# Rotary turn, score banks, order of maxima and roots in the differential attention of a two-block transformer kernel

## What is computed

```python
def rope(x, pos):                       # halves of 32 within each head of 64
    x1, x2 = xf[..., :half], xf[..., half:]
    return jnp.concatenate([x1 * cos - x2 * sin, x2 * cos + x1 * sin], axis=-1)

def diff_attention_group(q, k, v, pos, layer, lambdas, subln):
    q, k = rope(...), rope(...)         # 8 heads, each with two q and two k of 64
    # per block of 128 queries: two softmaxes over the keys up to the query's chunk of 64
    p1 = masked_softmax(q1 @ k1.T * scale, mask); p2 = masked_softmax(q2 @ k2.T * scale, mask)
    o = (p1 - lam * p2) @ v
    o = rms_norm_2(o, subln) * (1.0 - lam_init)
```

## Time and profile before

| what | value |
|---|---|
| median of 3 runs | 2726.69 us (2720.05 to 2731.51) |
| the profiled execution | 2719.96 us, span of its instructions 2718.2 us |
| mean granted clock of PE | 0.976 |
| PE busy (matmuls) | 2572.1 us, 95% of the span |
| PEld busy (weight loads) | 2022.0 us, 74% |
| DVE busy | 1305.1 us, 48% |
| ACT busy | 878.3 us, 32% |
| POOL busy | 1074.5 us, 40% |
| the chain that ended last | PE 78%, DVE 14%, ACT 4% of the span |

### The profile page before, as it was taken

One profiled execution on the slowest core, in us unless ns is written; L12 is line 12 of the kernel. 1 busy time (PEld: TensorE's weight loads), 2 busy tenths in 40 slices (PEclk: granted clock), 3 DMA queues, 4 the chain that ended last, 5 costly groups with the idle time before them and its releaser, 6 DMA issues.

```text
span 2718.2 us, 30446 instructions
## 1 busy us (share of the span) xinstructions
PE 2572.1 (95%) x11830; PEld 2022.0 (74%) x11830; DVE 1305.1 (48%) x2013; ACT 878.3 (32%) x1354; POOL 1074.5 (40%) x841
## 2 busy tenths in 40 slices
PE   7999999999999999989988999999997789999998
PEld 6878676888788888766766677888885666788886
DVE  4225677533433321585756654585126765533301
ACT  3443245322222222224444533322233243322221
POOL 4322243644454445343222235454452331544442
PEclk9999999999999999999999999999997889999999
DMA  3111122222222223211111122222320011222232
GB/s 134 66 55 63 50 74 72 95 97 94 93 90 95 95 90 94 92 62 60 49 47 47 47 70 99 93 93 91 97 97 30 21 40 39 97 94 94 93 94 74
DMA packets 62575, 209.45 MB, mean 77 GB/s; under 512 B 6880, under 2 KB 9312, under 8 KB 62304
## 3 DMA queue, kind: packets, MB, share of 16 engines
q1 hardware_dynamic: 61424, 204.11, 23.0%
q10 hardware_dynamic: 1008, 3.40, 0.3%
HBM read 205.38 MB, written 2.10 MB: 76 GB/s over the span
## 4 chain that ended last, share of the span: by engine, by line
PE 78%; DVE 14%; ACT 4%; issue 2%; POOL 1%; DMA 0%; DVEq 0%; ACTq 0%; SPq 0%; POOLq 0%
PE ps L609 22%; PE ps L610 22%; PE ps L611 22%; DVE T L2012 1%; PE ps L630 1%; ACT A L1475 1%; PE ps L632 1%; PE ps L631 1%; DVE A L2311 1%; DVE small L2157 1%; PE ps L920 1%; DVE A L1901 1%; POOL w_lo L567 1%; PE ps L737 1%; PE ps L739 1%
## 5 line engine op out<-in xcount | busy, mean ns | idle before, releaser
L567 POOL TENSOR_TENSOR w_lo<-w_raw,w_hi 128x512 fp32r<-128x512 f32 (+4 forms) x822 | 1047.1, 1298 | 1578.2 <-ACT w_hi L1214 1578.2
L609 PE MATMUL ps<-H,w_hi 128*128 128x512 f32 x1880 | 765.4, 407 | 39.5 <-POOL w_lo L567 19.6
L610 PE MATMUL ps<-H,w_hi 128*128 128x512 f32 x1880 | 750.7, 399 | 0.0
L611 PE MATMUL ps<-H,w_lo 128*128 128x512 f32 x1880 | 750.4, 399 | 0.0
L1214 ACT CAST w_hi<-w_raw 128x1024 fp32r<-128x1024 f32 (+4 forms) x411 | 401.9, 983 | 540.7 <-DMA w_raw<-in_weights_dram 535.1
L609 PEld LDWEIGHTS ps<-H,w_hi 128*128 128x128 f32 x1880 | 358.4, 191 | 139.2 <-issue 37.3
L609 PE MATMUL ps<-split,w_hi 128*128 128x512 f32 x1034 | 419.2, 405 | 11.8 <-POOL w_lo L567 5.8
L611 PEld LDWEIGHTS ps<-H,w_lo 128*128 128x128 f32 x1880 | 357.4, 190 | 87.2
L610 PEld LDWEIGHTS ps<-H,w_hi 128*128 128x128 f32 x1880 | 358.5, 191 | 81.9 <-issue 1.4
L610 PE MATMUL ps<-split,w_hi 128*128 128x512 f32 x1034 | 412.5, 399 | 0.0
L611 PE MATMUL ps<-split,w_lo 128*128 128x512 f32 x1034 | 412.1, 399 | 0.0
(11 more groups left out here) (395 smaller groups left out, 2493.7 us busy)
## 6 DMA issues: line engine op xcount, KB each, us to landing
w_raw<-in_weights_dram SPq DMA_DIRECT2D x323, 512.0 KB, 3.6
w_raw<-in_weights_dram SPq DMA_DIRECT2D x48, 448.0 KB, 3.2
w_raw<-in_weights_dram SPq DMA_DIRECT2D x22, 256.0 KB, 2.6
X<-in_xt_dram SPq DMA_DIRECT2D x4, 512.0 KB, 7.6
out_dram<-A SPq DMA_DIRECT2D x8, 256.0 KB, 2.2
w_raw<-in_weights_dram SPq DMA_DIRECT2D x12, 128.0 KB, 2.0
w_raw<-in_weights_dram SPq DMA_DIRECT2D x6, 192.0 KB, 2.3
A<-in_w_gates_dram ACTq DMA_DIRECT2D x1, 1024.0 KB, 5.6
```

The lines of the kernel that those rows point to most:

```text
L567: sub = nc.gpsimd.tensor_tensor(w_lo[:, p % NS, c], w_raw[:, p % NS, c], w_hi[:, p % NS, c].bitcast(F32), ALU.subtract)
L609: mm_(ps[:, bank, :], r(wh), xh, start=(k == 0), stop=False)
L610: mm_(ps[:, bank, :], r(wh), xl, start=False, stop=False)
L611: mm = mm_(ps[:, bank, :], r(wl), xh, start=False, stop=(k == kt - 1))
```

## The change

The rotary turn is made by ACT: behind the copy of a tile, four copies of 32 rows each from the bank to `ROPE_T`, each group from its neighbour's rows, with a scale of -1 or 1; ACT waits for the turn before (`s_roped`) first. PE's `rotate`, its matrix, and the "rot" items of the fill are gone; DVE's turn waits for the copies (`s_qc`) and reads `ROPE_T` in place of bank 2. The fills become 3 a step in the scan stage and 5, 5, 5, 4 in the attention. The scores of a step go to two of three banks (4, 5, 2) in turn, and `scores(c)` waits for the first exponential of the step before only. DVE takes the maxima of step c + 1 ahead of the normalising of step c. The head's root and reciprocal are exp(-0.5 ln(x)) on ACT, with a load of a table set that holds both functions ahead of the loop; DVE's reciprocal is gone. The root of the gate norm stays a square root at the same place, and a wait for its sums that `root` has anyway stands in front of it once more. In the last layer only counts of semaphores change.

```diff
@@ -405,6 +401,10 @@
         YG = parts_at(BW_AT, BW_AT + 2048)
         YC = parts_at(13312, 13312 + 2048)
         YD = parts_at(5120, 7168)
+
+        def map_bank(c, a):
+
+            return (4, 5, 2)[(2 * c + a) % 3]
 
         def h_tile(i):
             return H32[:, i // 8, i % 8, :]
@@ -514,14 +514,11 @@
         DONE_B = steps_done(FILL_B, PATTERN_B, 16)
 
         def dqkv_items(p):
-            name = f"dqk{p}"
-            return [((name, 0), 8), ((name, 1), 8), (("rot", 4 * p), 1), ((name, 2), 8), (("rot", 4 * p + 1), 1),
-                    ((name, 3), 8), (("rot", 4 * p + 2), 1), (("part", p), 12), (("rot", 4 * p + 3), 1),
-                    ((f"dv{p}", 0), 4)]
-
-        SSM_FILL = (3, 3, 3, 4)
+            return [((f"dqk{p}", n), 8) for n in range(4)] + [((f"dv{p}", 0), 16)]
+
+        SSM_FILL = (3,)
         DONE_SSM = steps_done(dqkv_items(0) + dqkv_items(1), SSM_FILL, 32)
-        DIFF_FILL = (5,)
+        DIFF_FILL = (5, 5, 5, 4)
         _items = dqkv_items(2)
         _items.insert(1, (("cols", 0), 0))
         _items.insert(3, (("spread", 0), 0))
@@ -862,13 +859,6 @@
             products_bc(6)
             products_bc(7)
 
-            def rotate(i):
-                p, n = divmod(i, 4)
-                pe.wait_ge(s_qc, i + 1)
-                if i >= 1:
-                    pe.wait_ge(s_rotf, i)
-                mm_(ps[:, 2, :], con("rot64"), QD[p][:, n, :], start=True, stop=True).then_inc(s_rot, 1)
-
             def fill_dqkv(p):
                 for n in range(4):
                     yield from units((f"dqk{p}", n), HX)
@@ -876,14 +866,7 @@
                         norm_cols("gate", 7)
                     if p == 2 and n == 1:
                         norm_spread("gate", 7, RTG)
-                    if n:
-                        rotate(4 * p + n - 1)
-                        yield
-                for u, _ in enumerate(token_units((f"dv{p}", 0), HX)):
-                    yield
-                    if u == 11:
-                        rotate(4 * p + 3)
-                        yield
+                yield from token_units((f"dv{p}", 0), HX)
 
             def segments(s):
                 pair, i = divmod(s, 4)
@@ -907,7 +890,7 @@
             segments(0)
             for s in range(32):
                 pair, i = divmod(s, 4)
-                n = SSM_FILL[s % 4]
+                n = SSM_FILL[s % len(SSM_FILL)]
                 run(fill, n // 2)
                 if s + 1 < 32:
                     segments(s + 1)
@@ -927,14 +910,14 @@
                 hh, w = head % 2, P * i + P
                 if c % 8 == 0:
                     pe.wait_ge(s_roped, 4 * p + 4)
-                if c >= 1:
-                    pe.wait_ge(s_ex, 2 * c)
+                if c:
+                    pe.wait_ge(s_ex, 2 * c - 1)
                 for a in range(2):
                     rows = slice(64 * a, 64 * a + 64)
-                    mm_(ps[:, 4 + a, 0:w], QD[p][rows, hh, P * i:P * i + P], QD[p][rows, 2 + hh, 0:w],
+                    mm_(ps[:, map_bank(c, a), 0:w], QD[p][rows, hh, P * i:P * i + P], QD[p][rows, 2 + hh, 0:w],
                         start=True, stop=False)
                 for a in range(2):
-                    mm_(ps[:, 4 + a, P * i:w], mask("ident"), mask("neg_chunk"), start=False, stop=True
+                    mm_(ps[:, map_bank(c, a), P * i:w], mask("ident"), mask("neg_chunk"), start=False, stop=True
                         ).then_inc(s_sc, 1)
 
             def value_sums(head):
@@ -1426,9 +1409,10 @@
 
             def copy_dqkv(tile):
                 name, t = tile
-                if name in ("rot", "part", "spread"):
+                if name == "spread":
                     return
                 if name == "cols":
+                    act.wait_ge(s_ncol, NORM["gate"] + 1)
                     root("gate", 7)
                     return
                 if name == "out2a":
@@ -1438,7 +1422,14 @@
                 finished(name, t)
                 if name == f"dqk{p}":
                     bank = USE[tile][0][0]
-                    link(nc.scalar.copy(QD[p][:, t, :], ps[:, bank, :]))
+                    i = 4 * p + t
+                    nc.scalar.copy(QD[p][:, t, :], ps[:, bank, :])
+                    if i:
+                        act.wait_ge(s_roped, i)
+                    for q in range(4):
+                        to, of = slice(32 * q, 32 * q + 32), slice(32 * (q ^ 1), 32 * (q ^ 1) + 32)
+                        turned = A_(ROPE_T[to], ps[of, bank, :], ACT.Copy, scale=1.0 if q % 2 else -1.0)
+                    link(turned)
                     act.sem_inc(bank_free[bank], 1)
                     act.sem_inc(s_qc, 1)
                 else:
@@ -1472,7 +1463,7 @@
                     act.wait_ge(s_tr, c - 1)
                 for a in range(2):
                     b = 50 + 4 * (c % 2) + a
-                    link(A_(EX[:, 2 * (c % 2) + a, 0:w], ps[:, 4 + a, 0:w], ACT.Exp,
+                    link(A_(EX[:, 2 * (c % 2) + a, 0:w], ps[:, map_bank(c, a), 0:w], ACT.Exp,
                             scale=0.125, bias=small[:, b:b + 1], accum_out=small[:, b + 2:b + 3]))
                     act.sem_inc(s_ex, 1)
 
@@ -1488,9 +1479,12 @@
                 act.sem_inc(s_og, 1)
 
             def head_root(head):
+
                 act.wait_ge(s_os, head + 1)
-                A_(cols[:, 12:16], ps[:, 7, 0:4], ACT.Sqrt, bias=con("eps"), scale=1.0 / P).then_inc(s_orms, 1)
-
+                link(A_(cols[:, 12:16], ps[:, 7, 0:4], ACT.Ln, bias=con("eps"), scale=1.0 / P))
+                A_(cols[:, 12:16], cols[:, 12:16], ACT.Exp, scale=-0.5).then_inc(s_or, 1)
+
+            nc.scalar.preload_act_table_set("natural_log_exp_and_others")
             exponentials(0)
             for c in range(32):
                 head, i = c // 4, c % 4
@@ -2107,17 +2101,16 @@
             def rope(i):
                 p, n = divmod(i, 4)
                 x = QD[p][:, n, :]
-                dve.wait_ge(s_rot, i + 1)
-                link(v.tensor_tensor(ROPE_T, ps[:, 2, :], SIN, ALU.mult))
-                dve.sem_inc(s_rotf, 1)
+                dve.wait_ge(s_qc, i + 1)
+                link(v.tensor_tensor(ROPE_T, ROPE_T, SIN, ALU.mult))
                 link(v.tensor_tensor(x, x, COS, ALU.mult))
                 link(v.tensor_tensor(x, x, ROPE_T, ALU.add))
                 dve.sem_inc(s_roped, 1)
 
             def ropes(tiles):
                 for name, i in tiles:
-                    if name == "rot":
-                        rope(i)
+                    if name.startswith("dqk"):
+                        rope(4 * int(name[-1]) + i)
 
             def gate_y(pair):
                 dve.wait_ge(s_yy, 4 * pair + 4)
@@ -2154,13 +2147,8 @@
                 b = 50 + 4 * (c % 2)
                 for a in range(2):
                     dve.wait_ge(s_sc, 2 * c + a + 1)
-                    link(v.tensor_reduce(small[:, b + a:b + a + 1], ps[:, 4 + a, 0:w], AX.X, ALU.max))
+                    link(v.tensor_reduce(small[:, b + a:b + a + 1], ps[:, map_bank(c, a), 0:w], AX.X, ALU.max))
                 v.tensor_scalar(small[:, b:b + 2], small[:, b:b + 2], -0.125, None, ALU.mult).then_inc(s_mx, 1)
-
-            def head_recip(head):
-                dve.wait_ge(s_orms, head + 1)
-                link(v.reciprocal(cols[:, 12:16], cols[:, 12:16]))
-                dve.sem_inc(s_or, 1)
 
             def head_out(head):
                 dve.wait_ge(s_osp, head + 1)
@@ -2177,8 +2165,8 @@
 
             def beside_diff(s):
                 for name, t in DONE_DIFF.get(s, []):
-                    if name == "rot":
-                        rope(t)
+                    if name.startswith("dqk"):
+                        rope(4 * int(name[-1]) + t)
                     if name == "cols":
                         rms("gate", RTG)
                     if name == "spread":
@@ -2192,21 +2180,18 @@
                 w = P * i + P
                 e1, e2 = EX[:, 2 * (c % 2), 0:w], EX[:, 2 * (c % 2) + 1, 0:w]
                 b = 50 + 4 * (c % 2)
+                if c < 31:
+                    maxima(c + 1)
                 dve.wait_ge(s_ex, 2 * c + 2)
                 link(v.reciprocal(small[:, b + 2:b + 4], small[:, b + 2:b + 4]))
                 link(v.tensor_tensor(small[:, b + 3:b + 4], small[:, b + 3:b + 4], small[:, 62:63], ALU.mult))
                 link(v.tensor_scalar(e1, e1, small[:, b + 2:b + 3], None, ALU.mult))
                 v.scalar_tensor_tensor(e1, e2, small[:, b + 3:b + 4], e1, ALU.mult, ALU.add).then_inc(s_pn, 1)
                 beside_diff(c - 1)
-                if c < 31:
-                    maxima(c + 1)
-                if i == 1 and head:
-                    head_recip(head - 1)
                 if i == 3 and head:
                     head_out(head - 1)
             beside_diff(31)
             dve.wait_ge(s_pn, 32)
-            head_recip(7)
             head_out(7)
             beside_diff(32)
             add_to_x("out2b", "ffn2", lambda k: ("norm_ffn_2", k))
```

18 lines of the change are left out of this document (7 added, 11 removed).

## The result

| | before | after |
|---|---|---|
| median of the runs, us | 2726.06 | **2750.77** (2749.93 to 2754.11) |
| ratio, 95% interval | | 1.0099 [1.0079, 1.0119] |
| span of the profiled run, us | 2718.2 | 2752.3 |
| scan stage, us | 122.8 | 124.4 |
| attention, us | 226.8 | 258.8 |

The account below looks back on a forecast made before the run. TensorE was taken as the bound before the attention; in the attention, what ends its waits decides. Scan stage -5.0 us and attention +5.7 us gave +0.7 us, so 2727 us, range 2708 to 2746 us.

Parts of the forecast that it names:

- Part 1: Both stages: rotation leaves TensorE, 7.6 us less each; scan stage, with 3.2 us of turn waits, -5.0 us.
- Part 2: Attention: with three score banks and earlier maxima, `s_ex` waits after the first go, -14.9 us; the first shortens by 0.6.
- part 3: Attention: with maxima of the next step first, transposes wait for normalising, +23.6 us (bounds 0 and 35).
- part 5: Attention: roots by ln and exp keep 16 table loads, costing 0 to 1 us; DVE's ended waits already counted.
- Part 4: Attention: turns waiting for quarters 3 us, gate norm's spread 1.5, a fill's bank 1.3; together +5.8 us (bounds 0 and 14).
- Rival 1: Attention: transposes don't wait, -32 us in all, 2695 us; chance 0.15 for a gain over 13.6 us.
- Rival 2: Both stages: DVE and GpSimd collide on the turn (5.3 us), +23 us, 2750 us; chance 0.15, including a lowered clock.

Follow-up runs that it names:

- e1: Changed kernel with DVE's maxima of the next step put back behind normalising and the work beside: 2736.3 us, ratio 1.0046.
- e8: Changed kernel with one 128-row copy in place of the four 32-row quarter copies, halves not swapped: 2750.3 us, ratio 1.0091.
- e3: Kernel before with only the rotation moved to ScalarE's quarter copies and the new fills: 2747.5 us, ratio 1.0088.
- e10: Kernel before with the rotation on ScalarE and new fills, plus maxima moved behind normalising and ahead of the turn: 2721.4 us, ratio 0.9984.
- e2: Kernel before with only DVE's maxima of the next step moved ahead of normalising: 2737.9 us, ratio 1.0053.
- e5: Kernel before with only the heads' roots changed to ln and exp on ACT: 2706.2 us, ratio 0.9935.
- e12: Changed kernel with GpSimd's subtractions cut to 64 of 512 columns for 22 weight panels, low parts left out: 2727.7 us, ratio 1.0011.

## Why the prediction was wrong

The stages show it: scan forecast at -5.0 us, measured +1.6 (+0.1 to +0.3 in the runs with the same turn at full clock); attention forecast at +5.7, measured +32.0.

In the attention the sum had PE's idle time rise by 13.3 us (-0.6 - 14.9 - 0.6 + 23.6 + 5.8); it rose by 20.1 (23.9 to 44.0). It had PE's busy time fall by 7.6 us; it rose by 11.9 (202.88 to 214.78). So 19.5 of the 26.3 us missed in this stage are busy time, and of the steps the one that failed is the clock: the forecast keeps it as it was and gives it no term, and the new waits brought it down, which lost about 15 us more than before (1.9 us of the 19.5 are the size of a rotation, below). The other 6.8 us are in the main waits: the transposes 2.7 above the forecast, the gate norm 3.1 and the fill's bank 2.4 above, a wait for the new root of 1.5 us (L945) that had no term, less the 3 us put on quarters that did not come.

**Part 1, rotation and turn.** Mis-sized in three terms. At full clock before and in e1, PE's busy time in the scan stage fell by 5.7 us (120.89 to 115.18), not 7.6: 0.71 us a rotation, not the 0.95 from start to start. The turn itself was right, 3.3 us forecast and 3.17 by its three means (755, 870 and 1547 ns). The quarters were not: 0.59 each and 2.39 for four where I had 2.1 with the link and 0.1 us of overlap at each. I had set the wait at 0.4 us a tile; it was 1.1 in six of eight tiles, 6.4 us. e8 settles that the quarters cause it. In the attention I put 3 us on 8 turns waiting for quarters, and in the changed kernel that wait is 0.3 us, for a reason that the working doesn't have: the maxima ahead of it wait longer. I had asked who waits for the turn, and not what stands behind and ahead of it on DVE. In the old order the maxima stand behind it, and there the turn costs 28.7 us (e3), 25.5 of them by order alone (e10). What the turn costs in the order of the change was not run by itself.

**Part 2, banks.** Wrong attribution. The -14.9 us of `s_ex` waits did go, but part 3 does it without the bank (e2), and part 5 takes off half of the 20.4 (e5). With the third bank in the old order 22.5 us stay (e1). The saving was counted once, correctly, but credited to an edit that isn't needed for it. The wait at the start did not get 0.6 us shorter: 5.5 before, 5.5 after.

**Part 3, maxima first.** Right in place and total, 23.6 us forecast, 26.3 measured, 23.3 in e2. The single terms were each some 0.3 us too long: undisturbed waits are 0.35, 0.79 and 0.91 us at c%4 = 1, 2 and 3 where I had 0.63, 1.11 and 1.20. In the step at 1433 the chain took 3.13 us (1433.16, the end of the scores, to 1436.29) and not 3.27, and the fills covered 2.34 and not 2.16. The collisions made up the total: 17.5 us with the subtractions cut in e12. That the total came out near is in part luck.

**Part 4, beside.** 5.8 us forecast. The wait for the gate norm's spread measured 4.6 us and the one for the fill's bank 3.7, against 1.5 and 1.3; the quarters 0.3, against 3.

**Part 5, roots.** The loads came as forecast, eight of each, on ACT in both stages together:

```profile
L1484 ACT ACT_TABLE_LOAD x8 | 10.3, 1283 | 0.1
L1485 ACT ACT_TABLE_LOAD x8 | 10.3, 1283 | 0.1
```

The place of this part in the sum was right: "those waits mattered only through the `s_ex` waits already counted", and with the maxima first only the one at the start is left for it to take off. Its value by itself was missed: 11.8 us of gain in the attention on the kernel before, 15.8 by the medians (e5), of which PE's shorter `s_ex` waits are 10.2. Half of the saving booked under the banks was to be had from this part alone, with none of the costs.

**The clock.** It had no term of its own. I set it aside with one row, 15.8 busy us of 20 at a clock of 1.00, and put "the many new waits lower the granted clock" into a rival at 0.15. Its loss grew by 16.2 us (20.7 - 4.5; 15.4 by stretches of 1 us). What e2 shows is that many waits alone don't do it: 24 at the transposes, 1 us on average, left it at 0.98, and past the start its only fall stands behind the longest, 1.86 us. The falls stand at single waits. In the changed kernel the 6 us behind each of the waits of 1.97 (1443.4), 2.32 (1467.1), 2.55 (1508.2), 2.69 (1553.4) and 3.68 us (1584.0) lose 1.7 us to the half level (0.28 x 6), as behind the second and the fourth:

```profile
1467.10:1473.10 6.00, 5.98 (x28) 4.66 (x28) 0.82 (x4) 1.43 (x6) 2.32 (x2) 0.72 0.01 3
...
1553.40:1559.40 6.00, 5.98 (x27) 5.02 (x28) 1.94 (x6) 0.48 (x1) 0.00 (x0) 0.72 0.10 16
```

Four more make up the 20.5 us: 3.4 in the wait at the start (5.5 us; it is there before, too), 3.4 behind another wait of 2.69 us (1400.1), 3.4 that began ahead of the end of the gate norm's 4.60 (1417 to 1425), and 1.6 behind one of only 1.31 us (1606.6). It is no rule by length: before, a wait of 2.92 us (1431.70) was followed by

```profile
1432.00:1436.00 4.00, 4.00 (x28) 3.17 (x26) 2.32 (x9) 1.43 (x5) 0.00 (x0) 1.00 0.00 0
```

What tells the two cases apart is open.

**The rivals.** Rival 1 (no waits) didn't occur. Rival 2 named the time, 2750 us, and the two agents, GpSimd and the clock, but in the wrong place, so that its time came true by luck: its turns of 5.3 us took 3.17 on average, the scan stage has 6.4 us of waits and not 17, and e8 puts those down to the quarters. The collisions that counted were with the operations of the maxima and of normalising. I had bounded exactly that at "some 0.4 us more" a step in part 3; it is 1.0 to 1.9 us at five places, and the clock on top.

The Trainium skill (SBUF — State Buffer, Who interferes with whom) says that a DVE instruction with two SBUF inputs, or a `tensor_scalar` in its two-port mode, and a GpSimd instruction that reads SBUF lock each other out for a whole instruction, while `tensor_reduce` never contends. The traces agree: L2187 ends with the second subtraction, at 1465.96 us against 1465.94 (it takes 1.11 us, each of the two about 1.25), L2151 goes from 0.17 to 0.73, and the maxima beside the start of the first keep their 1.42 us. By that rule the price of a collision is up to one whole subtraction, however small the DVE operation is; I had used it for the turn's 512-column operations alone.

## What to carry to other kernels

When an engine's queue is reordered, list for every moved step what now stands behind it as well as who waits for it, and test the order in between: normalise, maxima, beside took 34 us off this change with two lines moved. Give a saving to the edit that makes it by doing each alone; here the edit that looked like a mere replacement, the roots, was the only one that by itself made the kernel faster (the third bank was not tried by itself). Small operations that come onto the critical engine's path must be priced with what runs beside them. Where an edit puts new waits on PE, give the clock a term: here single waits of 1.3 to 3.7 us were followed by 1.6 to 3.4 us of loss in seven places of the changed kernel, and one of 2.9 us before the change by none.

## What the hardware showed that I had not expected

A copy of 32 rows by 512 columns from PSUM costs ScalarE as much as one of 128 rows, and four in a row take 2.39 us, with no overlap where two 512-wide exponentials took 1.26. The groups of the quarters in the changed kernel (both stages) and of e8's one copy (scan stage), with times, busy us and mean ns:

```profile
L1431 ACT ACTIVATE A<-ps 32x512 f32<-32x512 f32 x64 | 37.7, 588 | 0.8
```

```profile
L1429 ACT ACTIVATE A<-ps 128x512 f32<-128x512 f32 x8 | 4.9, 607 | 0.0
```

A DVE operation on a single column grew from 0.16 to 1.11 us beside a GpSimd subtraction. A single PE wait of 2.3 us was followed by a stretch at the half level that lost another 1.7 us, with matmuls of 0.63 us in place of 0.40.
